# Issuing the second pass's activation and gate loads from ScalarE's queue instead of SyncE's

## The reference

```python
expert = jnp.take_along_axis(cand_i, best_j, axis=-1)      # (tokens, 8, 16) of 16384
gate = jax.nn.softmax(best_s, axis=-1)
pre = jnp.einsum('thkd,td->thk', u[expert], xb)
act = jax.nn.gelu(pre, approximate=False) * gate
return jnp.einsum('thk,thkd->td', act, v[expert])          # then residual and a final rms_norm
```

## Time and profile before

| | |
|---|---|
| time, median of 3 runs | 1946.37 us |
| lowest and highest | 1932.54 and 1950.42 us |
| time of the profiled execution | 1944.54 us |
| its span, first to last instruction | 1942.7 us |
| mean granted TensorE clock | 0.952 |
| PE busy | 1824.1 us (94%) |
| DVE busy | 1456.2 us (75%) |
| ACT busy | 773.7 us (40%) |
| POOL busy | 636.7 us (33%) |
| moved by DMA | 484.52 MB |

### The profile page before, as it was taken

One profiled execution on the slowest core, in us unless ns is written; L12 is line 12 of the kernel. 1 busy time (PEld: TensorE's weight loads), 2 busy tenths in 40 slices (PEclk: granted clock), 3 DMA queues, 4 the chain that ended last, 5 costly groups with the idle time before them and its releaser, 6 DMA issues.

```text
span 1942.7 us, 26511 instructions
## 1 busy us (share of the span) xinstructions
PE 1824.1 (94%) x9787; PEld 1556.6 (80%) x9787; DVE 1456.2 (75%) x2722; ACT 773.7 (40%) x1536; POOL 636.7 (33%) x408
## 2 busy tenths in 40 slices
PE   6999999999999989999899999968999999999997
PEld 6998666679999889999899899966676676766664
DVE  4334666635578877989999999857787787687887
ACT  4112555443344433333677787422222222222222
POOL 0001100000000022333222365545575576575572
PEclk9999699768999999999999999989999999999999
DMA  6223000001222478888788799999999999989996
GB/s 240 76 87 132 25 1 1 1 3 49 72 72 72 167 245 306 303 297 292 249 278 294 269 383 381 391 404 390 399 393 375 402 381 366 401 335 405 400 408 233
DMA packets 156080, 484.52 MB, mean 249 GB/s; under 512 B 15200, under 2 KB 56160, under 8 KB 152240
## 3 DMA queue, kind: packets, MB, share of 16 engines
q1 hardware_dynamic: 98992, 270.92, 37.9%
q0 software_dynamic: 56528, 208.28, 28.9%
q10 hardware_dynamic: 432, 3.64, 0.5%
HBM read 422.61 MB, written 59.90 MB: 248 GB/s over the span
## 4 chain that ended last, share of the span: by engine, by line
PE 64%; DVE 18%; DMA 11%; issue 4%; ACT 2%; POOL 1%; SPq 0%; DVEq 0%; ACTq 0%; POOLq 0%
PE ps L939 15%; PE ps L917 15%; PE ps L587 10%; PE ps L854 5%; PE ps L948 5%; DMA g_in<-gates_scattered 5%; PE ps L683 3%; DVE hot L1639 3%; DMA raw<-w_tiles 3%; DVE w_lo L1262 3%; DMA v_buf<-v_rows 2%; PE ps L905 2%; DVE ring L1658 2%; PE ps L674 2%; PE ps L724 2%
## 5 line engine op out<-in xcount | busy, mean ns | idle before, releaser
L917 PE MATMUL ps<-md_hi,w_hi 128*128 128x384 f32 x1024 | 359.9, 351 | 44.7 <-DVE w_lo L1262 44.5
L567 POOL DMA_INDIRECT ring<-u_rows,idx_a x128 | 202.3, 1580 | 444.0 <-DVE dots L1658 324.1
L917 PE MATMUL ps<-md_lo,w_hi 128*128 128x384 f32 x1024 | 347.0, 339 | 0.0
L917 PE MATMUL ps<-md_hi,w_lo 128*128 128x384 f32 x1024 | 346.9, 339 | 0.0
L1262 DVE TENSOR_TENSOR w_lo<-raw,w_hi 128x1024 fp32r<-128x1024 f32 x176 | 215.5, 1225 | 92.8 <-ACT w_hi L1192 66.1
L567 POOL DMA_INDIRECT ring<-v_rows,idx_a x128 | 222.3, 1737 | 130.5 <-DVE acc L1666 102.4
L1658 DVE CUSTOM_DVE_ANT_0 ring<-ring,x_n 128x1024 f32<-128x1024 f32 x192 | 231.0, 1223 | 13.9 <-DMA ring<-u_rows,idx_b 11.7
L917 PEld LDWEIGHTS ps<-md_hi,w_hi 128*128 128x128 f32 x1024 | 195.4, 191 | 53.7 <-DVE w_lo L1262 52.8
L1666 DVE SCALAR_TENSOR_TENSOR acc<-ring,actg,acc 128x1024 f32<-128x1024 f32 x188 | 234.6, 1283 | 4.4 <-DMA ring<-v_rows,idx_a 4.4
L939 PE MATMUL ps<-w_hi,p_hi 128*128 128x512 f32 x576 | 195.2, 421 | 21.3 <-DVE w_lo L1722 21.2
L917 PEld LDWEIGHTS ps<-md_lo,w_hi 128*128 128x128 f32 x1024 | 195.6, 191 | 0.0
(11 more groups left out here) (250 smaller groups left out, 3393.0 us busy)
## 6 DMA issues: line engine op xcount, KB each, us to landing
raw<-w_tiles SPq DMA_DIRECT2D x176, 512.0 KB
v_buf<-v_rows SPq DMA_DIRECT2D x128, 512.0 KB
activated<-act_st SPq DMA_DIRECT2D x128, 192.0 KB
gates_scattered<-g_st SPq DMA_DIRECT2D x24, 1024.0 KB
g_in<-gates_scattered SPq DMA_DIRECT2D x32, 768.0 KB
act_in<-activated SPq DMA_DIRECT2D x32, 768.0 KB, 13.8
kv_t<-qkv ACTq DMA_DIRECT2D x3, 1184.0 KB, 7.5
xh<-x_t SPq DMA_DIRECT2D x8, 296.0 KB, 6.2
```

What stands on the lines that cost most here:

```text
L567: pool.indirect_dma_start(ring[slot][:], None, u_rows if table == "u" else v_rows, bass.IndirectOffsetOnAxis(ap=idx, axis=0)).then_inc(gat ...
L917: mm = nc.tensor.matmul(ps[:, slot, 0:ND], w[:, slot, kc, :], x[:, kc, :], start=(kc == 0 and j == 0), stop=(kc == KC - 1 and j == 2))
```

## The change

The two loading helpers move out of SP's program and take the queue as an argument. In the second pass the activation loads (from group 2 on) and the gate loads (from group 1 on) are issued by ACT, between its casts; SP issues only the v tiles there. Group 0's gates and the first two groups of activations stay with SP in the first pass. What each load waits for is kept; SP's wait on `act_stored` for the last activations moves to ACT, ahead of its first cast.

```diff
+        def load_gates(queue, grp, piece):
+            buf, b0 = grp % 2, piece * (N_GB // 4)
+            n = GL_TILES * GB_TOK
+            queue.dma_start(g_in[buf][:, b0:b0 + N_GB // 4].rearrange("p b i t -> p b (i t)"),
...
+        def load_acts(queue, grp):
+            queue.dma_start(act_in[grp % 3][:].rearrange("p j t -> p (j t)"),
+                         act_dram[grp * P:(grp + 1) * P, :]).then_inc(act_in_s[grp % 3], 16)
...
             for i in range(4, V_SLOTS):
                 load_v(i)
-            for s in act_stored:
-                sp.wait_ge(s, 16 * (N_EXP // 4))
-            load_acts(2)
             for i in range(N_EXP):
                 if i + V_SLOTS < N_EXP:
                     load_v(i + V_SLOTS)
-                if i % 4 == 0 and 4 <= i < N_EXP - 8:
-                    sp.wait_ge(v_done, i)
-                    load_acts(i // 4 + 2)
-                if i % 16 in (0, 3, 6, 9) and i < N_EXP - 16:
-                    if i >= 16:
-                        sp.wait_ge(p_made, i // 16 * 16)
-                    load_gates(i // 16 + 1, i % 16 // 3)
...
+            for s in act_stored:
+                act.wait_ge(s, 16 * (N_EXP // 4))
+            load_acts(act, 2)
             p_high(0)
             v_high(0)
             p_high(1)
...
                 if i + 2 < N_EXP:
                     v_high(i + 2)
+                if i % 4 == 0 and 4 <= i < N_EXP - 8:
+                    act.wait_ge(v_done, i)
+                    load_acts(act, i // 4 + 2)
+                if i % 16 in (0, 3, 6, 9) and i < N_EXP - 16:
+                    if i >= 16:
+                        act.wait_ge(p_made, i // 16 * 16)
+                    else:
+                        act.wait_ge(u_done, N_EXP)
+                    load_gates(act, i // 16 + 1, i % 16 // 3)
```

More of the change, by code:

```diff
@@ L406, in bass_hybrid_step @@
         FIN = [(4, 64), (3, P), (0, P), (1, P), (2, P)]
+        def load_gates(queue, grp, piece):
+            buf, b0 = grp % 2, piece * (N_GB // 4)
+            n = GL_TILES * GB_TOK
+            queue.dma_start(g_in[buf][:, b0:b0 + N_GB // 4].rearrange("p b i t -> p b (i t)"),
+                         g_dram[b0 * P:(b0 + N_GB // 4) * P, grp * n:(grp + 1) * n].rearrange(
+                             "(b p) n -> p b n", p=P)).then_inc(g_in_s[buf], 16)
+        def load_acts(queue, grp):
+            queue.dma_start(act_in[grp % 3][:].rearrange("p j t -> p (j t)"),
+                         act_dram[grp * P:(grp + 1) * P, :]).then_inc(act_in_s[grp % 3], 16)
         @block.sync
@@ L426, in _ @@
                 load_tile(n)
[L428 to L437, removed]
             def load_v(i):
@@ L484, in _ @@
                 if G_END + 2 <= i < G_END + 6:
-                    load_gates(0, i - G_END - 2)
+                    load_gates(sp, 0, i - G_END - 2)
                 if i == G_END + 6:
@@ L488, in _ @@
                         sp.wait_ge(s, 32)
-                    load_acts(0)
-                    load_acts(1)
+                    load_acts(sp, 0)
+                    load_acts(sp, 1)
                 if G_END + 7 <= i < G_END + 11:
```

## The result

The changed kernel takes 1991.94 us (median of 6 runs, 1982.67 to 1998.05), the kernel before 1942.53 (median of its 6 runs beside it); the ratio is 1.0252, 95% interval 1.0215 to 1.0289. That is some 49 us. The profiled execution took 1982.67 us. It is 38 us over that of before (1944.54) and not 49, since its first pass ended 11 us earlier (the last Gelu at 1317.4 against 1328.7 us; in the stretch from 200 to 400 us PE's clock was 0.85 in place of 0.80). So positions of the second pass are compared from its own start.

What follows compares the result with a forecast made beforehand. It took PE's pace to bound the second pass, with stalls on late gates behind full DMA engines (396 GB/s). 1944.5 plus 5.0 seam plus 15.7 gate stalls less 1.5 for the last 16 tiles gave 1964 us; range 1934 to 1982.

Steps and rivals of the forecast that it cites:

- the slow case: Rival for the second pass: full 3.4 us gate delay in seven groups, activations later too; 1976 us and above, chance 0.24.
- The seam: Between first and second pass: ACT waits for the last activation stores before its first cast, PE idles longer; +5.0 us.
- The order of bytes: Second pass DMA queues: v tiles served at once put 1.36 MB more ahead of gates; landing 0 to 3.4 us later, 1.7 taken.
- the upper end: Largest delay forecast for the last gate piece's landing: 1.36 MB more v bytes ahead, 3.4 us at 396 GB/s.
- gathers' brake: q0 cannot run ahead of q10, so up to two or three gathers are left for later, giving back 0 to 3.4 us.
- The clock: Three split tiles after PE's idle at each group's start run slower than at full clock; 1.8 us a group.
- The number of groups: Between tiles 4 and 112: seven groups load gates and lose 6.0 us each, 42 us where 26.3 are lost now.
- When they are issued: Second pass gate issues: last piece 1448.4 in place of 1449.5, middle ones up to 4 us earlier; no gain, q10 not empty.
- ACT's time: Some 58 loads issued by ACT in the second pass, 0.43 us each, 25 us in 590; costed at nothing.
- gates land when they do now: Rival: gathers left behind make up for the v tiles, stalls stay, only 5.0 us come on top; 1949 us, chance 0.26.
- ahead of need: Rival: short queues, gates land early and second-pass stalls vanish, leaving only the byte count; 1935 us, chance 0.12.
- The bound by bytes: Second pass without stalls: 16 tiles need 29.1 MB, 72.5 us at 401 GB/s against 70.8; 1.7 us a group.

Runs made afterwards that it cites:

- large-packet run: Changed kernel with gates laid out in DRAM so that a load's packet is 6144 bytes in place of 1024: 1924.67 us, 0.9942 of the kernel before.
- two controls: Changed kernel, new gate layout, padded back to smaller packets: 1024 bytes 1991.37 us (1.0263 of the kernel before), 3072 bytes 1934.71 us (0.9948).
- pair of swapped kernels: Kernel before with ACT issuing v tiles, SP activations and gates: 1955.1 us; the same with activation loads one tile later: 1972.67 us; side by side.
- swapped kernel with equally late loads: Kernel before with ACT issuing v tiles, SP activations and gates, activation loads waiting for v_done i + 1 instead of i: 1972.02 us (1.0156), repeated 1972.67 (1.016).

## Why the prediction was wrong

*The result* was outside the range (1934 to 1982), in the direction of the slow case, which I gave 0.24.

*The seam*: +5.0 forecast, 5.15 us in the trace; right. The kernel with it alone is 5 us slower, but its interval doesn't exclude zero.

*The mechanism*: right in kind. v tiles served at once (8.0 us to landing), turns one to one among three queues, more bytes ahead of the last gate piece, the wait on `g_in` growing. The large-packet run and its two controls show that it is this that costs.

*The failed step is "The order of bytes"*: "Later by 0 to 3.4 us; I take the middle, 1.7". It was later by 6.6 us (67.6 against 61), since 2.60 MB more went by where the upper end had 1.36. By queue:
- v tiles: 1.91 MB more (7.89 against 5.98), forecast 1.36. I had counted them up to the old landing, but each microsecond of delay admits more.
- q10: 0.62 MB more (6.13 against the 5.51 of four pieces and three activation groups), forecast nothing. It is part of a fourth group, issued behind the last gate piece and yet through before all of that piece had landed.
- Gathers: 0.08 MB more (12.69 against 12.61). I had counted on up to 1.36 MB less.

How the gathers' brake was lost is seen at the old landing, 61 us after the first piece's issue, window 1404.9:1465.9:

```profile
DMA packets 8539, 24.15 MB, mean 396 GB/s; under 512 B 675, under 2 KB 3578, under 8 KB 8535
...
q0 software_dynamic: 3234, 11.76, 49.1%
q1 hardware_dynamic: 1897, 6.91, 29.0%
q10 hardware_dynamic: 3404, 5.42, 24.2%
```

By then the gathers had given way by 0.85 MB (11.76 against 12.61), inside what was forecast. But 274 of q10's 3678 packets were still to go; at 95 in 2 us, as in the short window above, that is an estimated 5.8 us more, and it took 6.6. In these the gathers caught up. The upper end, 3.4, was no upper end: I closed the range with the tile count of the old stretch, and a sum of bytes doesn't say when the queue with the most turns to take is through.

*The clock*: 1.8 us a group forecast. The six groups lost 1.9 to 3.0 us by it, 2.5 in the mean, so this term too was small, by 0.7 us a group. How long PE idles doesn't settle it. Timeline of the changed kernel at tile 64:

```profile
1645.94 1.19 PE L929 MATMUL ps<-w_hi,p_hi 128*128 128x512 f32 x2 [9.99 <-DVE w_lo L1724]
```

and timeline and chain of the kernel before, at the same tile:

```profile
1630.42 1.19 PE L939 MATMUL ps<-w_hi,p_hi 128*128 128x512 f32 x2 [3.45 <-DVE w_lo L1722]
...
1630.42 15.55 PE ps L939 x54
```

Behind the longer idle (9.99 us) the three split tiles take 14.48 us, 1.9 over full clock, and behind the shorter (3.45 us) 15.55, 3.0 over. Why stays open.

*The number of groups*: seven forecast, six seen; tile 16 came in time. So 42 us were forecast for tiles 4 to 112, and 68.9 were lost.

*When they are issued*: "this gains only if q10 is empty then" was right for the middle gate pieces. The last piece was forecast 1.1 us earlier and went 0.7 us later: 44.87 us after tile 16's start (1445.05 - 1400.18) in place of 44.19. The activation group's place just ahead of the first gate piece is no part of the change: the kernel before has it too. But it is worth something once the gates have a queue apart from v's: one tile more or less is 17.6 us (the pair of swapped kernels). No run tried that in the single queue.

*ACT's time* was costed at nothing. That is not settled. The changed kernel less the seam stands at 1.0252 - 0.0028 = 1.022, the swapped kernel with equally late loads at 1.016 (1.0107 to 1.0213), gates alone on ACT at 1.0228 (1.0169 to 1.0288). The intervals overlap, and no run separates what may be some 12 us. A path by ACT is there: before tile 32 the last gate piece stood behind a cast that waited 3.95 us for DVE, and DVE for activations. But it went only 0.7 us later by it. The traces show more of something else. The swapped kernel with the later load, first gate piece's issue to last one's landing, window 1401.9:1467.7, and two lines that follow each other in the timeline of ACT's loads:

```profile
DMA packets 9132, 26.02 MB, mean 395 GB/s; under 512 B 733, under 2 KB 3805, under 8 KB 9129
...
q10 hardware_dynamic: 1912, 6.96, 26.6%
...
v_buf<-v_rows ACTq DMA_DIRECT2D x12, 512.0 KB, 8.2
...
1454.76 0.33 ACTq L1237 DMA_DIRECT2D v_buf<-v_rows  x1
...
1468.29 0.33 ACTq L1237 DMA_DIRECT2D v_buf<-v_rows  x1
```

Twelve v tiles are issued there, none in the 13.5 us up to 1468.29, in which ACT's casts wait for DVE and DVE for the gates. In the changed kernel SP, which waits for free buffers alone, issues 15 in its window, and 26.75 MB go by and not 26.02. The 0.73 MB are 1.8 us at 396 GB/s, in six groups an estimated 11 us, about what the two kernels differ by. So the rest is rather v's issuer than the gates'; no run with that alone changed shows it.

*Rivals*: that gates land when they do now, 1949, and ahead of need, 1935, were both wrong. For the first, "q0 is empty by then anyway" was misread from a window behind the landing: in the kernel before q0 still moves 0.63 MB from 1466 to 1468 us and 0.44 MB from 1468 to 1470, and the landing is at 1471.39. The large-packet run shows what would have made the second one true. *The bound by bytes* in it (72.5 us for 16 tiles) was too pessimistic: with large packets PE keeps full pace over most groups at 402 to 410 GB/s.

*A page weighed*: the Trainium skill, DMA: Bandwidth & Descriptors, "Issuing engines are not separate DMA queues", has the choice of issuer save issue time and nothing else. The total rate agrees, it stayed at 396 GB/s. The time does not: here the same bytes over the same engines cost 2.5% more, through the order in which the queues are served, which that page's section "Queues, rings and completion order" gives.

## What to carry to other kernels

When the DMA engines are full, splitting a queue gives no bytes (396 GB/s before and after); it changes who is last. In one queue an urgent load stands ahead of all that is issued after it; in a queue of its own it shares turns with everything, and with small packets it is served worst. So count packets, not bytes, for each queue; let the stretch grow with the delay while you count; and before moving a load to another queue make its packets as large as its neighbours': the layout in DRAM did here what no choice of queue did.

## What the runs showed of the hardware

Turns are by packet and not by bytes also among three queues: 91, 97 and 95 packets in 2 us, with 0.37, 0.34 and 0.10 MB. Such counts don't show whether an engine goes on after each packet or after several of a queue. Raising the gate packets from 1024 to 3072 bytes took the landing of 768 KB from 24.5 to 11.8 us beside two queues of 4096-byte packets, and 6144 bytes to 9.7 us. Packets of one queue need not all be through in the order of issue: part of an activation group issued 12.7 us behind a gate piece (1457.75 and 1445.05) had been moved when that piece landed. Behind an idle of PE its next 54 matmuls took 1.8 to 3.0 us more than at full clock, at a granted clock of 0.50 in the first 5 us behind one of 8.95 us.
